# A two-block float32 transformer kernel: where the last weight splits, one stream's head features and the modulation matmuls are issued

## The reference

```python
sh1, sc1, g1, sh2, sc2, g2 = split(silu(c) @ ada_w[i] + ada_b[i], 6)       # 1024 -> 6144, also for c_ctx
h = rmsnorm(x, norm_mix[i]) * (1.0 + sc1) + sh1
# i == 0: differential attention, x attends to x and ctx, ctx to itself
p = softmax(q @ k.T / 8); a = p[0] - lam * p[1]; o = rmsnorm(a @ v, subln) * 0.8
# i == 1: neighbourhood attention of x (16 heads, bias and window mask), with the context as more keys
x = x + g1 * (o @ wo)
x = x + g2 * conv_ffn(rmsnorm(x) * (1.0 + sc2) + sh2, ...)
```

## Time and profile before

| | us |
|---|---|
| median of 3 runs | 3014.82 (3011.76 to 3021.93) |
| the profiled execution, its own time | 3020.77 |
| its span, first to last instruction | 3018.9 |
| PE busy | 2757.6 (91%) |
| DVE busy | 1729.8 (57%) |
| ACT busy | 1408.0 (47%) |
| POOL busy | 80.1 (3%) |

### The profile page before, as it was taken

How to read it: one execution, slowest core, us unless ns; L and a number is a source line. 1 busy time by engine, 2 the same in 40 slices (tenths; PEclk the granted TensorE clock), 3 DMA queues, 4 the chain that set the end, 5 groups by cost and what they waited for, 6 DMA issues and landing times.

```text
span 3018.9 us, 44994 instructions
## 1 busy us (share of the span) xinstructions
PE 2757.6 (91%) x17755; PEld 2222.6 (74%) x17755; DVE 1729.8 (57%) x2021; ACT 1408.0 (47%) x1693; POOL 80.1 (3%) x113
## 2 busy tenths in 40 slices
PE   6999788979999998788979999977999999989898
PEld 5877477767878886377867887844888887867686
DVE  4556634656545545734655555666677676554574
ACT  4444323434434433323444544455576674455573
POOL 0001000000000001000000000000000000011000
PEclk9999889989999999899989999987999999978899
DMA  5448801434454457801434454420444445431353
GB/s 193 180 168 290 332 2 58 147 140 154 181 196 177 172 194 277 317 3 58 147 146 157 193 188 161 171 95 1 155 177 184 181 167 194 180 120 59 128 182 125
DMA packets 74123, 479.09 MB, mean 159 GB/s; under 512 B 8894, under 2 KB 13084, under 8 KB 19824
## 3 DMA queue, kind: packets, MB, share of 16 engines
q1 hardware_dynamic: 60608, 440.43, 39.2%
q0 software_dynamic: 8752, 32.23, 3.0%
q10 hardware_dynamic: 4608, 4.20, 0.5%
HBM read 468.13 MB, written 2.13 MB: 156 GB/s over the span
## 4 chain that ended last, share of the span: by engine, by line
PE 78%; DVE 9%; DMA 4%; ACT 4%; DVEq 3%; issue 2%; ACTq 0%; POOL 0%; SPq 0%; POOLq 0%
PE ACC L401 64%; PE M L401 5%; PE TP L401 5%; PE TP L477 3%; DMA raw<-wstream 3%; DVE w_lo L1435 2%; ACT w_hi L970 1%; PE TP L671 1%; DMA PREV<-V 1%; DVE PR L1954 1%; ACT XX L1105 0%; DVE ST L1940 0%; DMA BIAS<-toe 0%; DVEq L1941 0%; PE TP L791 0%
## 5 line engine op out<-in xcount | busy, mean ns | idle before, releaser
L1435 DVE TENSOR_TENSOR w_lo<-raw,w_hi 128x2048 fp32r<-128x2048 f32 x371 | 841.7, 2290 | 449.3 <-ACT w_hi L970 421.9
L970 ACT ACTIVATE w_hi<-raw 128x2048 fp32r<-128x2048 f32 x371 | 703.2, 1916 | 430.8 <-DMA raw<-wstream 266.3
L401 PE MATMUL ACC<-w_hi,HA_hi 128*128 128x512 f32 (+1 forms) x2032 | 805.4, 396 | 27.9 <-DVE HA_lo L1507 13.9
L401 PE MATMUL ACC<-w_hi,HA_lo 128*128 128x512 f32 (+1 forms) x2032 | 795.7, 392 | 0.0
L401 PE MATMUL ACC<-w_lo,HA_hi 128*128 128x512 f32 (+1 forms) x2032 | 795.2, 391 | 0.0
L401 PEld LDWEIGHTS ACC<-w_hi,HA_hi 128*128 128x128 f32 x2032 | 387.8, 191 | 110.2 <-issue 21.0
L401 PEld LDWEIGHTS ACC<-w_hi,HA_lo 128*128 128x128 f32 x2032 | 386.9, 190 | 80.7
L401 PEld LDWEIGHTS ACC<-w_lo,HA_hi 128*128 128x128 f32 x2032 | 387.8, 191 | 76.6
L401 PE MATMUL ACC<-w_hi,FT_hi 128*128 128x512 f32 x616 | 245.1, 398 | 7.0 <-issue 7.0
L401 PE MATMUL ACC<-w_hi,FT_lo 128*128 128x512 f32 x616 | 243.3, 395 | 0.0
L401 PE MATMUL ACC<-w_lo,FT_hi 128*128 128x512 f32 x616 | 243.3, 395 | 0.0
(11 more groups left out here) (318 smaller groups left out, 3141.6 us busy)
## 6 DMA issues: line engine op xcount, KB each, us to landing
raw<-wstream SPq DMA_DIRECT2D x371, 1024.0 KB, 4.8
ADW<-wada SPq DMA_DIRECT2D x48, 1024.0 KB, 12.9
BC<-vecs POOLq DMA_DIRECT2D x19, 512.0 KB, 6.4
BIAS<-toe ACTq DMA_DIRECT2D x32, 128.0 KB, 2.8
BC<-mod_scr POOLq DMA_DIRECT2D x6, 512.0 KB, 5.9
PREV<-R POOLq DMA_DIRECT2D x4, 448.0 KB, 5.9
PREV<-K POOLq DMA_DIRECT2D x4, 448.0 KB, 6.7
PREV<-V POOLq DMA_DIRECT2D x4, 448.0 KB, 9.3
```

The lines of the kernel that those rows point to most:

```text
L401: return pe.matmul(*a, skip_group_check=True, **k)
L970: act.activation(w_hi[:, s, :], unit, ACT.Copy).then_inc(sem["hi_ready"], 1)
L1435: dve.tensor_tensor(w_lo[:, s, :], unit, w_hi[:, s, :].bitcast(F32), ALU.subtract).then_inc(sem["lo_ready"], 1)
```

## The change

Five edits.

1. `project` no longer calls `split(2)` after its last block. The two units are split in the attention instead, one at the end of iterations 26 and 28 of `attend_pair`, and one at the end of iterations 11 and 13 of `attend` (`LATE_SPLITS`), on ACT after `turned_probs`, on DVE after `output` or `mix`.
2. The head features of stream 0 are made in four iterations, 20 to 23, one group in each; the scaling in iterations 18 to 21.
3. In `attend_pair` one maximum of 128 x 2 x w takes the place of two of 128 x w, and one negation that of two. Both exponentials of a turn wait for it.
4. A modulation unit now holds all 2048 columns of one k-tile (`_units_wide`), so 8 units fill one group of 2048 columns in one bank, in three groups for each layer. Units 0 to 7 stand in the stage of the factors, in pairs; the other 16 in the four WKV turns, four in each, where two stood. There are 3 copies and 3 sums for each layer where 12 stood, the sums with eight selecting columns. ACT's copy of group 0 comes behind the last exponential, those of groups 1 and 2 in the second and the fourth WKV turn.
5. ACT's splits in the third and the fourth WKV turn wait until the modulation units whose slots they overwrite are used.

```diff
@@ -287,6 +287,7 @@
 A4 = [ACC[0][:, 0, :], ACC[0][:, 1, :], ACC[1][:, 0, :], ACC[1][:, 1, :]]
+MOD_BANK = (TP[0], A4[0], A4[1])
@@ -337,6 +338,7 @@
 ROOT_AT, SCALE_AT, TURN_AT = 17, 18, 20
+LATE_SPLITS = (26, 28), (11, 13)
@@ -586,27 +588,21 @@
             pe.wait_ge(sem["cc_ready"], c.next("cc_ready"))
-        mod_chunk(l, 0)
-        mod_chunk(l, 1)
-        mod_sums(l, 0)
+        mod_units(l, 0, 2)
-        mod_chunk(l, 2)
-        mod_sums(l, 1)
+        mod_units(l, 2, 4)
-        mod_chunk(l, 3)
-        mod_sums(l, 2)
+        mod_units(l, 4, 6)
-        for q in range(4, 8):
-            mod_chunk(l, q)
-            mod_sums(l, q - 1)
-        mod_sums(l, 7)
+        mod_units(l, 6, 8)
+        mod_sums(l, 0)
@@ -641,25 +637,24 @@
         block_wide(HB_hi, HB_lo, between=lambda: raw_half(0))
-    def mod_chunk(l, q):
-        if q in range(2, 8):
-            pe.wait_ge(sem["ada_copied"], 12 * l + q - 1)
-        bank = TP[q % 2] if q < 8 else A4[q % 2]
-        for part in range(2):
-            n = 2 * q + part
+    def mod_units(l, a, b):
+        for n in range(a, b):
+            group, k = divmod(n, 8)
+            bank = MOD_BANK[group]
-            for k in range(4):
-                last = mm(bank[32 * k:32 * k + 32, :], CB[:, 4 * part + k, :],
-                          ADW[:, ada_slot(l, n), 512 * k:512 * k + 512], start=part == 0, stop=part == 1)
+            for j in range(4):
+                last = mm(bank[32 * j:32 * j + 32, :], CB[:, k, :],
+                          ADW[:, ada_slot(l, n), 512 * j:512 * j + 512], start=k == 0, stop=k == 7)
-    def mod_sums(l, q):
-        pe.wait_ge(sem["ada_copied"], 12 * l + q + 1)
-        bank = M[1] if q < 8 else A4[2]
+    def mod_sums(l, group):
+        pe.wait_ge(sem["ada_copied"], 3 * l + group + 1)
+        bank = M[1] if group == 0 else A4[2]
-            last = mm(bank[:, 8 * q + 2 * f:8 * q + 2 * f + 2], ADAS[:, q % 2, P * f:P * f + P],
-                      K_[:, C_SEL:C_SEL + 2], start=True, stop=True)
+            at = 32 * group + 8 * f
+            last = mm(bank[:, at:at + 8], ADAS[:, group % 2, P * f:P * f + P],
+                      K_[:, C_SEL:C_SEL + 8], start=True, stop=True)
@@ -685,8 +680,12 @@
             if pair == 0:
-                mod_chunk(l, 8 + 2 * g + t)
-        mod_sums(l, 8 + 2 * g + t)
+                at = 8 + 4 * (2 * g + t)
+                mod_units(l, at, at + 4)
+        if (g, t) == (1, 0):
+            mod_sums(l, 1)
+        if (g, t) == (1, 1):
+            mod_sums(l, 2)
@@ -805,10 +804,13 @@
         last.then_inc(sem["o_ready"], 1)
+    def head_feature(s, g):
+        pe.wait_ge(sem["xn_ready"], c.next("xn_ready"))
+        turn(OUTS[s], 2, k0=2 * g)
-            pe.wait_ge(sem["xn_ready"], c.next("xn_ready"))
-            turn(OUTS[s], 2, k0=2 * g)
+            head_feature(s, g)
@@ -821,8 +823,8 @@
                 turn_probs(n, PAIR_TURNS[n][0], 1)
-            if n == TURN_AT:
-                head_features(0)
+            if 0 <= n - TURN_AT < KT // 2:
+                head_feature(0, n - TURN_AT)
@@ -1080,20 +1082,19 @@
         return t[:, :, 512 * j:512 * j + 512]
-    def mod_copies(a, b):
-        for q in range(a, b):
-            act.wait_ge(sem["ada_used"], c.next("ada_used", 2))
-            act.activation(ADAS[:, q % 2, :], (TP if q < 8 else A4)[q % 2][:, :], ACT.Copy) \
-                .then_inc(sem["ada_copied"], 1)
-    def wkv(n):
+    def mod_copy(l, group):
+        act.wait_ge(sem["ada_used"], ADA_UNITS * l + 8 * group + 8)
+        act.activation(ADAS[:, group % 2, :], MOD_BANK[group][:, :], ACT.Copy).then_inc(sem["ada_copied"], 1)
+    def wkv(l, n):
-        mod_copies(8 + n, 9 + n)
+        if n in (1, 3):
+            mod_copy(l, 1 + n // 2)
@@ -1109,6 +1110,7 @@
             if n >= 2 and j in (2, 3):
+                act.wait_ge(sem["ada_used"], ADA_UNITS * l + 16 + 4 * (n - 2) + 2 * (j - 1))
@@ -1152,22 +1154,17 @@
         for src, name in ([(AA, "vsig_ready")] if l else []) + [(T1, "sig_ready"), (AA, "asig_ready")]:
-            if name == "sig_ready":
-                mod_copies(0, 2)
-        mod_copies(2, 3)
-                    if n == 2:
-                        mod_copies(3, 8)
@@ -1176,9 +1173,10 @@
         act.activation(GAM[:, :], M[0][:, 0:32], ACT.Exp)
+        mod_copy(l, 0)
-            wkv(n)
+            wkv(l, n)
@@ -1234,7 +1232,8 @@
                 take_turned(*which)
-            split(2)
+            if j + 1 < len(turned):
+                split(2)
@@ -1264,7 +1263,8 @@
         for hb in range(2):
-            act.wait_ge(sem["max_ready"], c.next("max_ready"))
+            if biased or hb == 0:
+                act.wait_ge(sem["max_ready"], c.next("max_ready"))
@@ -1292,8 +1292,11 @@
                 root(16)
-            if n == TURN_AT:
-                features_plain(HA_hi, gain=COL[:, G_SUB:G_SUB + 1])
+            if 0 <= n - TURN_AT < KT // 2:
+                at = 2 * (n - TURN_AT)
+                feature_hi(HA_hi[:, at:at + 2, :], COL[:, G_SUB:G_SUB + 1])
+            if n in LATE_SPLITS[0]:
+                split(1)
@@ -1330,6 +1333,8 @@
                 turned_probs(n, 4, 2 * n + hb)
+            if n in LATE_SPLITS[1]:
+                split(1)
@@ -1663,19 +1668,25 @@
-            def mod_columns(l, w):
-                dve.wait_ge(sem["ada_sum"], c.next("ada_sum", 8 - 4 * w))
-                for m in ((0, 1, 2, 3), (4, 5))[w]:
+            def mod_columns(l, group):
+                dve.wait_ge(sem["ada_sum"], 3 * l + group + 1)
+                for m in (2 * group, 2 * group + 1):
+                if group != 1:
...
@@ -1781,6 +1792,7 @@
         mod_columns(l, 1)
+        mod_columns(l, 2)
@@ -1935,12 +1948,10 @@
             st0, w = 8 * (n % 2), T if PAIR_TURNS[n][0] else 2 * T
-            for hb in range(2):
-                dve.wait_ge(sem["sc_ready"], c.next("sc_ready"))
-                dve.tensor_reduce(ST[:, st0 + hb:st0 + hb + 1], A4[2 * (n % 2) + hb][:, 0:w], AX.X, ALU.max)
-                dve.drain()
-                ts(ST[:, st0 + 2 + hb:st0 + 3 + hb], ST[:, st0 + hb:st0 + hb + 1], -SCALE, None, ALU.mult) \
-                    .then_inc(sem["max_ready"], 1)
+            dve.wait_ge(sem["sc_ready"], c.next("sc_ready", 2))
+            dve.tensor_reduce(ST[:, st0:st0 + 2], ACC[n % 2][:, :, 0:w], AX.X, ALU.max)
+            dve.drain()
+            ts(ST[:, st0 + 2:st0 + 4], ST[:, st0:st0 + 2], -SCALE, None, ALU.mult).then_inc(sem["max_ready"], 1)
@@ -1965,9 +1976,10 @@
             rates(16, P, NORM_EPS, at=16 * s)
-        def scaled_heads(s):
-            dve.wait_ge(sem["rs_ready"], c.next("rs_ready"))
-            for k in range(KT // 2):
+        def scaled_heads(s, groups=range(KT // 2)):
+            if 0 in groups:
+                dve.wait_ge(sem["rs_ready"], c.next("rs_ready"))
+            for k in groups:
@@ -1984,12 +1996,15 @@
                 head_rates(0)
-            if n == SCALE_AT:
-                scaled_heads(0)
-            if n == TURN_AT:
-                e.skip_turns(TURN_AT + 1)
-                features_plain(HA_hi, HA_lo, gain=COL[:, G_SUB:G_SUB + 1])
-        e.skip_turns(31 - TURN_AT)
+            if 0 <= n - SCALE_AT < KT // 2:
+                scaled_heads(0, (n - SCALE_AT,))
+            if 0 <= n - TURN_AT < KT // 2:
+                at = 2 * (n - TURN_AT)
+                e.skip_turns(TURN_AT + 1 if at == 0 else 1)
+                feature_lo(HA_lo[:, at:at + 2, :], HA_hi[:, at:at + 2, :], COL[:, G_SUB:G_SUB + 1])
+            if n in LATE_SPLITS[0]:
+                split(1)
+        e.skip_turns(31 - TURN_AT - (KT // 2 - 1))
@@ -2304,6 +2321,11 @@
     return w.reshape(2, 4, P, m, 512).transpose(3, 0, 2, 1, 4).reshape(2 * m, P, UNIT)
+def _units_wide(w):
+    return w.reshape(KT, P, 3, UNIT).transpose(2, 0, 1, 3).reshape(3 * KT, P, UNIT)
```

More of the change, by code:

```diff
@@ L52 @@
 C_SEL = C_CHUNK + 2
-NCONST = C_SEL + 2
+NCONST = C_SEL + 8
 def constants():
@@ L75, in constants @@
         out[:, C_CHUNK + c] = (a // CHUNK == c) * np.float32(-DECAY)
-    for s in range(2):
-        out[:, C_SEL + s] = a % 32 == 16 * s
+    for n in range(8):
+        out[:, C_SEL + n] = a == 16 * n
     return out
@@ L1664, in mask @@
                 return K_[:, col:col + width].unsqueeze(1).broadcast_to([P, n, width])
[L1666 to L1678 removed]
+            def mod_columns(l, group):
+                dve.wait_ge(sem["ada_sum"], 3 * l + group + 1)
+                sums = (M[1] if group == 0 else A4[2])[:, 32 * group:32 * group + 32] \
+                    .rearrange("p (f j s) -> p f j s", f=4, j=4)
+                for m in (2 * group, 2 * group + 1):
+                    at = G_ADA + 48 * l + 8 * m
+                    bias = COL[:, at:at + 8].rearrange("p (a f) -> p f a", f=4).unsqueeze(3).broadcast_to([P, 4, 2, 2])
+                    if m in (2, 5):
+                        dst = GT[:, l, m // 3, :, :].rearrange("p s (a f) -> p f a s", f=4)
+                    else:
```

(10 more changed lines are left out.)

8 lines of the change are left out of this document (removed).

## The result

The changed kernel takes 3021.6 us (median of 10 runs, 3018.9 to 3028.1), the kernel before beside it 3013.5 (median of 10). The ratio is 1.0029, with a 95% interval of 1.0016 to 1.0042: 0.3% slower. I had forecast 3021.2 us, 6.4 us more than the median known then.

The account below looks back on a forecast made before the run. PE was taken as busy nearly throughout, but not the limit in the touched stages; DVE paces the first attention. Terms -14.7 + 10.0 + 12 - 8.5 + 4.5 - 12.1 + 15.2 = +6.4 gave 3021.2 us, range 3006 to 3037.

Parts of the forecast that it names:

- the iterations 26 and 28: First attention, stream 0: with a late split in them, the time between maxima was to be about 7.5 us.
- the second Gram product: WKV turns, on DVE: 4.8 us from the first to the second Gram product, where it was 2.9.
- The waits for `w_hi`: Second attention, late splits: DVE was to wait about 4.5 us for ACT's half of each.
- DVE's wait in the factor stage: Factor stage: DVE's waits were to fall under 0.3 us, from idle times of 8.52 and 5.20 us.
- 1, the barrier: End of each projection stage: without two splits PE starts 6.4 us earlier, first scores 0.95 us shorter; -14.7 us in all.
- 2, the late splits: Attentions: splits delay DVE, which sets the turn; +10.0 us in the first, +12 in the second (9 to 16).
- rival (a): Half clock behind the second attention's late splits (+6) and in four-unit WKV groups (+5): sum +17, 3032 us; chance 0.25.
- 3, the joint maximum: First attention: one maximum for both heads saves 0.30 us a turn; -8.5 us, bounds -4 and -9.7.
- 4, the head features: First attention: spread over four iterations, DVE waits anew in each; +4.5 us, between +3.4 and +7.
- 5, the factor stage: Factor stages: the third exponential no longer stands behind modulation copies, so DVE's idle time nearly vanishes; -12.1 us.
- 6, the WKV turns: WKV turns: two extra units make everything behind 1.9 us later in each of 8 turns; +15.2 us, bounds 0 and +28.
- Rival (c): WKV turns absorb the extra units where PE later waits for DVE: 0 to +4, sum -9 to -5, 3008 us; chance 0.16.

Follow-up runs that it names:

- late_early: Kernel before with the barrier splits moved into the attentions, DVE's in iterations 26, 28 and 11, 13, ACT's one iteration earlier; 3013.1 us, ratio 0.9984.
- wkv_dup: Kernel before with the two modulation units of each WKV turn multiplied twice at the same place; 3019.2 us, ratio 0.9997.
- joint_only: Kernel before with only the joint maximum for both heads in the first attention; 3011.1 us, ratio 0.9989.
- wkv_gapdup: Kernel before with each WKV turn's two units multiplied again in PE's later wait between the XX transposes, the sums moved behind it; 3021.1 us, ratio 1.0004.
- late_only: Kernel before with only the last two splits of each projection stage moved to attention iterations 26, 28 and 11, 13; 3029.5 us, ratio 1.0045.

## Why the prediction held, point by point

The time came out as forecast, and most terms did; two were off by 4 us and more, in opposite directions. The signs that I had named are there for the barrier (PE's wait 1.2 us), the joint maximum (3.27 us between maxima), the iterations 26 and 28 (7.7 and 7.9 us from one reciprocal of DVE to the next) and the second Gram product (4.6 us behind the first on DVE, 2.9 before). The waits for `w_hi` in the second attention (4.5 forecast) and DVE's wait in the factor stage (under 0.3 forecast, 1.4 measured) came out longer.

- **1, the barrier.** Forecast -6.4 and -0.95 in each layer. PE's wait went from 7.75 to 1.21 us, 6.54 less, and the first 8 score instructions from 3.79 to 1.99. Right.
- **2, the late splits.** In the first attention DVE waits 2.82 us and works 2.29, 5.1 us as worked out (5.0), and `late_early` confirms how that price is made up: with ACT's half ahead, only DVE's 2.3 remain. In the second attention I had 12, with 9 and 16 as bounds, and this term was mis-sized: from the last step ahead of the first split to the end, both kernels that have the splits take 16.1 us more than the kernel before. The mean of their two stages, 99.3 us, is 15.8 above the mean of the seven without, 83.5, and the changed kernel's own trace has 15.7 over that of before. The first wait was 5.26 us, the second 8.26 and not 4.5: the first stall, 6.7 us of idle PE, put PE on the half clock, and so ACT reached its second half later. This is rival (a)'s mechanism, true in this place; its price there, 12 + 6, was 2 us too much. It is also what the Trainium skill, TensorE: Matmul & The Clock Gate, section "Why this matters for your kernels", says of gaps between bursts; by it I had worked out 16, and the trace agrees with that and not with my 12.
- **3, the joint maximum.** -8.5 forecast, -8.0 measured; the maximum of 1024 columns takes 1.22 us as extrapolated.
- **4, the head features.** +4.5 forecast, +3.7 by the stage, but only 1.3 to 2.7 in the iterations that the edit touches. A little overpriced.
- **5, the factor stage.** -12.1 forecast, -12.5 in the trace; of DVE's waits for an exponential there, one of 1.4 us is left in each layer. The last sums are level with DVE's end, as allowed for.
- **6, the WKV turns: the mis-sized term.** +15.2 forecast as 1.9 us in each of 8 turns. The extra 1.72 us stand on the path as I said, and the second Gram product is that much later. But the three profiled kernels with four contiguous units have 358.6 to 362.0 us, in the mean 359.8, which is 6.4 above the 353.4 of those without; the trace of the changed kernel has 4.6 more than that of before. The bounds were 0 and 28. The step that failed is "everything behind is 1.9 us later", in each turn: it took the later matmuls at the speed that they had, and in the turn shown above half-clock stretches that cost 2.2 and 1.6 us went and one of 1.5 us came. `wkv_dup` shows that the added matmuls alone bring this about; why they raise the clock isn't shown. PE has no less idle time in that turn: by the windows above it is idle for 44.34 - 38.89 = 5.45 us before and for 43.84 - 37.49 = 6.35 in the changed kernel. Rival (c) was nearer with its 0 to +4 for this part, though its total of -9 to -5 was wrong, and its reason, slack in the chain, isn't what the turn shows. Rival (a) had expected a lower clock in this stage; it rose, from 0.89 and 0.91 to 0.95 and 0.94.

The sum of my terms was +6.4, in which part 6 was 10.6 too high (15.2 - 4.6) and part 2 some 4 too low. By the traces the terms are -12.5, +4.6, -13.1, +4.3 and +15.7, together -1.0 us, and 3.7 more lie in stages that the change doesn't touch. The medians are 8.1 us apart. With the means over kernels for WKV and the second attention it is -12.5 + 6.4 - 13.1 + 4.3 + 15.8 = +0.9, and 4 to 12 us of the measured difference (its interval is 5 to 13 us) have no stage that I can name. One profile of each kernel doesn't settle it: the stretch from the end of layer 1's turns to the end of the first projection has 530.2 to 531.5 us in some kernels and 532.9 to 533.8 in others, with and without the change. That the forecast came within 0.4 us of the median is thus in part luck.

## What to carry to other kernels

Work that is taken out from in front of a barrier is worth its full length only if it is put where its own engine waits; in a pipelined turn whose pace that engine sets it costs its length again, and if its first half is on another engine, that engine's lag too. Put the halves in different iterations, each in a wait seen in the trace, and look first behind the last turn. A stall of several us in front of PE is to be priced twice, once as itself and once as a stretch of half-clock matmuls behind it. Matmuls that are added to a chain of short waits can cost less than their length, because the half-clock stretches move; here they cost from an eighth (`wkv_dup`) to a half of it, and the rule for other kernels isn't known. When an experiment fills a wait, look in the trace at what else its edit moved.

## What the runs showed of the hardware

The same WKV turn, with the same instructions, took 40.6 to 44.3 us by where PE's half-clock stretches fell: the second turn of layer 0 ran at the full clock from end to end in `joint_only`, 40.58 us at 1.00, where others have about 44 at 0.88 to 0.91:

```profile
406.20:446.78 40.58, 34.89 (x808) 30.62 (x808) 14.01 (x30) 11.44 (x21) 0.00 (x0) 1.00 0.01 3
```

Two more units in a turn raised the clock of the stage to 0.95 when they stood in one block with the first two (`wkv_dup`), but only to 0.92 when they stood in a gap behind, with the sums behind them (`wkv_gapdup`, 178 us for each layer). The same matmuls gave a different clock by their place, and I have not found what decides it. In the second attention the clock was 0.53 in the mean over the 35.6 us around and behind the first late split, nearly all of it at the lower level; in `late_only` the same stretch was as long to 0.1 us.
